# A twelve-stage transformer kernel: the hand-over between two stages in another order, with one weight split of each hand-over in two parts

## The chip, the cores and the metric

The kernel runs on one core of one Trainium2 chip. The metric is the device time of one launch in microseconds; the time given for the kernel before is the median of 3 runs. A profiled execution of the same program gives a trace of every engine, and all durations below are from that one execution.

## The reference, cut to what matters

Twelve residual stages run on x of 256 tokens by 1024 channels, all in float32. Each stage is a normalization, a mixer or a feed-forward block, and a second normalization before the residual addition:

```python
def rms_norm(x, g):
    y = x * lax.rsqrt(jnp.mean(x * x, axis=-1, keepdims=True) + RMS_EPS)
    return y * g

def swiglu(x, w_gate, w_up, w_down):
    return (jax.nn.silu(x @ w_gate) * (x @ w_up)) @ w_down

# first block, for each of two layers
x = x + rms_norm(attention(rms_norm(x, pre), ...), post)
x = x + rms_norm(swiglu(rms_norm(x, pre), ...), post)
# second block, for each of two layers
x = x + 0.5 * rms_norm(swiglu(rms_norm(x, ng[0]), ...), ng[1])
x = x + rms_norm(mixer(rms_norm(x, ng[2])) @ w_out, ng[3])
x = x + rms_norm(memory_xattn(rms_norm(x, ng[4]), mem_n, ...), ng[5])
x = x + 0.5 * rms_norm(swiglu(rms_norm(x, ng[6]), ...), ng[7])
```

The order of the stages is na, ffn, dil, ffn, ffn, rwrt, xa, ffn, ffn, dsa, xa, ffn. The two xa stages attend to a second, normalized input (mem).

## The kernel before, in words

**Weights.** All weights come as one stream of 302 chunks of 128 x 2048 float32 (1 MB each), which SyncE loads into a ring of three buffers (`raw`). A matmul of float32 accuracy is made of three fast ones: every operand is split in a high part and the rest. ScalarE makes the high part of a chunk, `whi` (`act_hi`, L294), and VectorE the rest, `wlo = raw - whi` (`dve_lo`, L301). The first three chunks are split in `first_lo` (L306). `mm3` (L225 to L227) and `mm3t` (L231 to L233) then issue `whi*hi`, `whi*lo` and `wlo*hi`. The semaphores `w_hi` and `w_lo` count split chunks, `w_used` counts chunks that TensorE is done with. The split of chunk g+3 is issued by ScalarE and VectorE in the place of chunk g. SyncE reloads a raw buffer once `w_lo` says that its chunk was split (L1879).

**A stage.** First come the projection chunks: bank `pj` gets two tiles of 128 x 256 per chunk, each a sum over eight k slices of the normalized input (`xh`, `xl`, 128 channels each). Then the output phase (`out_pe`): `AR` (the block's result, high and low parts) times the output weights, two k slices per chunk, summed in four banks `acc[0..3]` of 128 x 512, which are two token halves t by two channel halves h.

**The hand-over between two stages**, which the change touches, happens eleven times. In the order of the data:

1. `last_chunk` in `out_pe` finishes the banks one after another. ScalarE squares and sums each (`post_act`, L406). VectorE runs `post_dve`: `scaled(b)` (L416) multiplies a bank by the gain, `mean(t)` (L421) adds up a half's sums, GpSimd raises them to the power -0.5 (L349), and `added(t, h)` (L428) adds the scaled bank to the residual `xt`. The semaphore `x` of the next stage counts these four additions.
2. TensorE transposes `xt` to channels by tokens (`turn_pe`, L339), one k slice and one token half at a time; `tr` counts finished slices. ScalarE makes `xh` of slice k from it (`pre_hi`, L370, count `hi`), VectorE makes `xl` (`pre_lo`, L392, count `lo`). The mean over channels is applied to the products later, so it is not in this chain: ScalarE squares `xt` (`pre_sq`, L378), VectorE makes the mean (`pre_mean`, L397), GpSimd the power (L344), and TensorE broadcasts it (`bcast_pe`, L355).
3. `slices_pe` runs the first two projection chunks of the next stage slice by slice, so that it can start when the first slice is there: for each k, four calls of `mm3` (two chunks, two halves), that is 12 matmuls of 128 x 256. After slices 0 to 3 it issues the transposes of slices 4 to 7.

All engines run their instructions strictly in the order of the program, and wait at semaphores. VectorE's order in the output phase and the hand-over is: the `wlo` splits of the output phase (`out_dve`), `scaled(0)`, `mean(0)`, `scaled(1)`, `scaled(2)`, `added(0,0)`, `mean(1)`, `scaled(3)`, `added(1,0)`, `added(0,1)`, `added(1,1)`, `pre_lo` of slices 0 to 3, a split of a whole weight chunk, `pre_lo` of slices 4 and 5, `pre_mean`, `pre_lo` of slices 6 and 7.

The last split in `out_dve` is that of chunk 1 of the next stage's projection, the second of the two that `slices_pe` uses; the split inside `post_dve` is that of chunk 2.

**The two hand-overs into an xa stage** differ. There the first chunk of the xa stage multiplies the normalized mem, so its 48 matmuls are used to fill TensorE's waits (`first_keys`, calls of `fill`), and `slices_pe` has only one chunk (n = 1), with a fill after slice 3. In these two, VectorE also makes the low part of the eight mem slices (`mem_dve`, L795) just behind its last split in `out_dve`.

Of the kernel before, what the change touches and what calls it, by code (L numbers as in the profile page):

```python
# [8 lines left out]
P = 128  # L9
D = 1024  # L10
T = 256
KT = D // P
# [6 lines left out]
F32 = mybir.dt.float32  # L19
F32R = mybir.dt.float32r  # L20
I32 = mybir.dt.int32
ALU = mybir.AluOpType
# [61 lines left out]
def build_program(nc, stages, wstream, xin, xtok, memin, memtok, vecs_d, gains_d, consts_d, rpb, small, out):  # L84
    NCH = n_chunks(stages)
    with ExitStack() as ctx:
# [5 lines left out]
        def sem(name):  # L92
            if name not in sems:
                sems[name] = ctx.enter_context(nc.semaphore(name))
            return sems[name]
# [89 lines left out]
        w_hi = sem("w_hi")  # L185
        w_lo = sem("w_lo")
        w_used = sem("w_used")
        pj_free = sem("pj_free")
        x_in = [sem(f"x_in{i}") for i in range(3)]
        vchain = sem("vchain")  # L190
# [105 lines left out]
        def dve_lo(dve, g, gs):  # L296

            if isinstance(g, int) and g + 3 >= NCH:
                return
            dve.wait_ge(w_hi, g + 4)  # L300
            nc.vector.tensor_tensor(wlo[:, gs, :], raw[:, gs, :], whi[:, gs, :].bitcast(F32),  # L301
                                    ALU.subtract).then_inc(w_lo, 1)

        def first_lo(dve, j):
            dve.wait_ge(w_hi, j + 1)
            nc.vector.tensor_tensor(wlo[:, j, :], raw[:, j, :], whi[:, j, :].bitcast(F32),  # L306
                                    ALU.subtract).then_inc(w_lo, 1)

        def out_dve(dve, w, nk, beside=lambda dve, c: None):
            def body(c, g, gs, it, p, ps):  # L310
                dve_lo(dve, g, gs)
                beside(dve, c)
            chunk_loop(dve, w, nk // 2 - 1, body, peel=1, last=True)

# [22 lines left out]
        def turn_pe(pe, t, k):  # L337

            return nc.tensor.transpose(acc[k % 4][:, (k // 4) * T + t * P:(k // 4) * T + (t + 1) * P],  # L339
                                       xt[:, t, k * P:(k + 1) * P], ident)  # L340
# [69 lines left out]
        def post_dve(dve, w, tag, half, nxt):  # L410

            tmp = [Sb[:, 0, :], Sb[:, 1, :], PTb[:, 0, :], PTb[:, 1, :]]

            def scaled(b):
                dve.wait_ge(*at(tag, "sq", b + 1))
                link(dve, nc.vector.scalar_tensor_tensor(tmp[b], acc[b][:, :], half * D ** 0.5,  # L416
                                                         GB[:, (b % 2) * 512:(b % 2 + 1) * 512], ALU.mult, ALU.mult))

            def mean(t):
                dve.wait_ge(*at(tag, "sq", 2 * t + 2))  # L420
                nc.vector.scalar_tensor_tensor(ss[:, 6 + t:7 + t], ss[:, 2 * t:2 * t + 1], D * EPS,  # L421
                                               ss[:, 2 * t + 1:2 * t + 2], ALU.add, ALU.add)\
                    .then_inc(sg(tag, "mv"), 1)

            def added(t, h):
                dve.wait_ge(*at(tag, "rs", t + 1))
                x = xt[:, t, h * 512:(h + 1) * 512]
                nc.vector.scalar_tensor_tensor(x, tmp[2 * t + h], rsc[:, t:t + 1], x, ALU.mult, ALU.add)\  # L428
                    .then_inc(sg(nxt[0], "x"), 1)

            dve.wait_ge(*at(tag, "g", 16))
            scaled(0)
            mean(0)
            scaled(1)
            scaled(2)
            added(0, 0)
            mean(1)
            scaled(3)
            added(1, 0)
            added(0, 1)  # L440
            added(1, 1)
            if nxt[1]:
                for k in range(4):
                    pre_lo(dve, *nxt, k)
            dve_lo(dve, w.g, w.g % 3)
            w.g += 1
            if nxt[1]:
                for k in range(4, 6):
                    pre_lo(dve, *nxt, k)
                pre_mean(dve, nxt[0])  # L450
                for k in range(6, KT):
                    pre_lo(dve, *nxt, k)
                bcast_dve(dve, nxt[0], rP[:, :], nxt[2])

        def out_pe(pe, w, nk, lo_at, tag, ready, nxt, beside=lambda pe, c: None, fill=lambda pe, n, g=0: None,
# [3 lines left out]
            def last_chunk(g):  # L459
                gs, k0 = g % 3, (nk - 2 + kt0) % nk  # L460
                pe.wait_ge(w_lo, g + 1)
                pe.wait_ge(*at(tag, ready, nk))
                for b in range(4):
                    t, h = divmod(b, 2)
                    for kk in range(2):
                        wk = slice(kk * D + h * 512, kk * D + (h + 1) * 512)
                        x = mm3t(acc[b][:, :], whi[:, gs, wk], wlo[:, gs, wk], AR[:, k0 + kk, t * P:(t + 1) * P],
                                 AR[:, lo_at + k0 + kk, t * P:(t + 1) * P], False, kk == 1)
                    if b == 3:
                        x.then_inc(w_used, 1)  # L470
                    else:
                        x.then_inc(sg(post, "ob"), 1)
                if not nxt:
                    return
                fill(pe, 3, g + 1)
                pe.wait_ge(*at(nxt, "x", 1))
                pe.wait_ge(*at(post, "sq", 3))
                for k in range(3):
                    turn_pe(pe, 0, k)
                fill(pe, 4)  # L480
                pe.wait_ge(*at(nxt, "x", 2))
                for k in range(4):
                    if k == 3:
                        turn_pe(pe, 0, k)
                    last = turn_pe(pe, 1, k)
                    last.then_inc(sg(nxt, "tr"), 1)
                fill(pe, 4)

            def body(c, g, gs, it, p, ps):
# [24 lines left out]
        def proj_pe(pe, w, n, tiles):  # L514
# [7 lines left out]
                    after_chunk.pop(0)()  # L522
            chunk_loop(pe, w, n, body, peel=min(n, len(after_chunk)), is_proj=True)

        def slices_pe(pe, w, n=2, fill=lambda pe, n: None):

            tag = split_tag.pop()
            for c in range(n):
                pe.wait_ge(w_lo, w.g + c + 1)
                pe.wait_ge(pj_free, w.p + c + 1)  # L530
            for k in range(KT):
                pe.wait_ge(*at(tag, "lo", k + 1))
                for c in range(n):
                    for half in range(2):
                        last = mm3(pj[(w.p + c) % 3][:, half * T:(half + 1) * T], (w.g + c) % 3, half * KT + k,
                                   xh[:, k, :], xl[:, k, :], k == 0 and half == 0, k == KT - 1)
                    if k == KT - 1:
                        last.then_inc(w_used, 1)
                if k < 4:
                    if k == 0:  # L540
                        pe.wait_ge(*at(tag, "x", 4))
                    turn_pe(pe, 0, k + 4)
                    turn_pe(pe, 1, k + 4).then_inc(sg(tag, "tr"), 1)
                if k == 3:
                    fill(pe, 5)
            w.g += n
            w.p += n
            bcast_pe(pe, tag, rsc[:, 2:4])
# [1604 lines left out]
```

## Time and profile before

| | |
|---|---|
| Median of 3 runs | 2385.3 us (2384.82 to 2387.32) |
| Profiled execution, its own time | 2383.44 us |
| Its span in the trace | 2381.3 us |
| TensorE busy | 2134.6 us (90%), 14826 matmuls |
| VectorE busy | 1442.8 us (61%) |
| ScalarE busy | 946.6 us (40%) |
| GpSimd busy | 27.4 us (1%) |
| Granted TensorE clock, mean | 0.938 |
| DMA | 341.44 MB, mean 143 GB/s |

The span is the time from the first to the last instruction in the trace; the execution's own time is 2.1 us longer. Busy is the time in which an engine ran at least one instruction. The granted clock is 1.00 at 2.4 GHz and 0.50 at 1.2 GHz.

### The profile page before, as it was taken

The numbers are of one execution on the slowest core, as the hardware profiler recorded it, in microseconds if no ns is written. First come the engines' busy times: TensorE is split into PE (matmuls) and PEld (weight loads), VectorE is DVE, ScalarE is ACT, GpSimd is POOL, SyncE is SP. The second block draws the span as 40 slices with busy tenths as digits, with TensorE's granted clock in tenths as the row PEclk, the third lists the DMA queues.
The fourth block names the chain that finished last, engine by engine and source line by source line (L and its number), as shares of the span: only waits on it lengthen the run. The fifth ranks groups of instructions, "written<-read, shape, count | busy, mean of one in ns | idle before, by whom it ended". The sixth has DMA issues, their size and how long they took to land.

```text
span 2381.3 us, 36838 instructions
## 1 busy us (share of the span) xinstructions
PE 2134.6 (90%) x14826; PEld 1958.8 (82%) x14826; DVE 1442.8 (61%) x1982; ACT 946.6 (40%) x1249; POOL 27.4 (1%) x46
## 2 busy tenths in 40 slices
PE   5779999999999999999982998799999996597998
PEld 5668988989878997998972888699799886386997
DVE  4646755555565764774687736577467456565773
ACT  4334444333344444443421315444344333354442
POOL 0000000000000000000000000000000000000000
PEclk8899999999999999999996978899999988898999
DMA  6214554443323554455540004255545542142553
GB/s 270 107 62 150 186 203 151 159 142 107 124 89 115 194 187 175 162 191 196 194 148 11 1 36 151 80 194 178 202 144 192 194 167 103 44 154 70 193 197 112
DMA packets 49787, 341.44 MB, mean 143 GB/s; under 512 B 5776, under 2 KB 6544, under 8 KB 9616
## 3 DMA queue, kind: packets, MB, share of 16 engines
q1 hardware_dynamic: 45648, 324.36, 38.0%
q10 hardware_dynamic: 4032, 15.53, 1.8%
q8 instruction: 82, 1.34, 0.2%
q14 instruction: 25, 0.20, 0.0%
HBM read 338.82 MB, written 1.05 MB: 143 GB/s over the span
## 4 chain that ended last, share of the span: by engine, by line
PE 82%; DVE 12%; issue 2%; ACT 2%; DMA 1%; POOL 0%; DVEq 0%; SPq 0%; POOLq 0%; ACTq 0%
PE pj L225 16%; PE pj L226 16%; PE pj L227 16%; PE acc L231 6%; PE acc L233 6%; PE acc L232 6%; PE acc L569 2%; PE pj L233 2%; PE pj L232 2%; PE pj L231 2%; PE acc L561 2%; PE mb L578 2%; DVE xt L428 1%; DMA raw<-in_wstream 1%; DVE sm L604 1%
## 5 line engine op out<-in xcount | busy, mean ns | idle before, releaser
L301 DVE TENSOR_TENSOR wlo<-raw,whi 128x2048 fp32r<-128x2048 f32 x299 | 685.0, 2291 | 406.5 <-ACT whi L294 406.5
L225 PE MATMUL pj<-xh,whi 128*128 128x256 f32 x3024 | 876.3, 290 | 20.9 <-DVE wlo L306 12.9
L226 PE MATMUL pj<-xl,whi 128*128 128x256 f32 x3024 | 866.8, 287 | 0.0
L227 PE MATMUL pj<-xh,wlo 128*128 128x256 f32 x3024 | 866.3, 286 | 0.0
L294 ACT ACTIVATE whi<-raw 128x2048 fp32r<-128x2048 f32 x299 | 570.5, 1911 | 549.7 <-PE acc L233 239.4
L225 PEld LDWEIGHTS pj<-xh,whi 128*128 128x128 f32 x3024 | 592.4, 196 | 27.4 <-issue 27.4
L226 PEld LDWEIGHTS pj<-xl,whi 128*128 128x128 f32 x3024 | 592.6, 196 | 0.0
L227 PEld LDWEIGHTS pj<-xh,wlo 128*128 128x128 f32 x3024 | 591.8, 196 | 0.0
L231 PE MATMUL acc<-whi,AR 128*128 128x512 f32 x688 | 275.3, 400 | 9.4 <-DVE AR L1768 4.4
L232 PE MATMUL acc<-whi,AR 128*128 128x512 f32 x688 | 273.9, 398 | 0.0
L233 PE MATMUL acc<-wlo,AR 128*128 128x512 f32 x688 | 273.5, 397 | 0.0
L738 ACT ACTIVATE AR<-F 128x256 f32 (+1 forms) x132 | 55.2, 418 | 376.8 <-DVE F L719 376.8
L231 PEld LDWEIGHTS acc<-whi,AR 128*128 128x128 f32 x688 | 130.8, 190 | 41.7 <-issue 4.6
L233 PEld LDWEIGHTS acc<-wlo,AR 128*128 128x128 f32 x688 | 130.5, 190 | 31.6
L232 PEld LDWEIGHTS acc<-whi,AR 128*128 128x128 f32 x688 | 130.7, 190 | 30.8
L561 PE MATMUL acc<-F 64*128 64x128 f32 (+2 forms) x320 | 77.1, 407 | 70.1 <-DVE sm L604 33.4
L561 PEld LDWEIGHTS acc<-F 64*128 64x128 f32 (+1 forms) x320 | 48.6, 213 | 84.7 <-DVE sm L604 39.4
L722 DVE TENSOR_TENSOR AR<-F,AR 128x256 f32 (+1 forms) x132 | 56.2, 426 | 100.5 <-ACT AR L738 100.5
L640 ACT ACTIVATE Sb<-Sb,sm 128x256 f32<-128x256 f32 (+1 forms) x96 | 55.3, 576 | 142.7 <-DVE sm L604 142.4
L711 DVE TENSOR_TENSOR F<-pj,rP 128x512 f32<-128x512 f32 x132 | 90.6, 686 | 0.2
L231 PE MATMUL pj<-whi,xh 128*128 128x256 f32 (+1 forms) x304 | 86.5, 285 | 0.0
L232 PE MATMUL pj<-whi,xl 128*128 128x256 f32 (+1 forms) x304 | 86.5, 284 | 0.0
(324 smaller groups left out, 2063.0 us busy)
## 6 DMA issues: line engine op xcount, KB each, us to landing
raw<-in_wstream SPq DMA_DIRECT2D x302, 1024.0 KB, 4.8
F<-in_gains ACTq DMA_DIRECT2D x12, 512.0 KB, 5.4
F<-in_rpb SPq DMA_DIRECT2D x4, 1024.0 KB, 17.5
F<-in_memtok ACTq DMA_DIRECT2D x2, 1024.0 KB, 4.8
F<-in_memin ACTq DMA_DIRECT2D x2, 1024.0 KB, 7.7
F<-in_small ACTq DMA_DIRECT2D x1, 1536.0 KB, 6.6
F<-in_xin SPq DMA_DIRECT2D x2, 512.0 KB, 6.2
xt<-in_xtok SPq DMA_DIRECT2D x1, 1024.0 KB, 11.3
```

The costliest lines, as they stand in the source:

```text
L225: nc.tensor.matmul(o, wh, k_hi, start=first, stop=False, skip_group_check=True)
L226: nc.tensor.matmul(o, wh, k_lo, start=False, stop=False, skip_group_check=True)
L227: return nc.tensor.matmul(o, wl, k_hi, start=False, stop=last, skip_group_check=True)
L231: nc.tensor.matmul(o, k_hi, wh, start=first, stop=False, skip_group_check=True)
L232: nc.tensor.matmul(o, k_lo, wh, start=False, stop=False, skip_group_check=True)
L233: return nc.tensor.matmul(o, k_hi, wl, start=False, stop=last, skip_group_check=True)
L294: nc.scalar.activation(whi[:, gs, :], raw[:, gs, :], ACT.Copy).then_inc(w_hi, 1)
L301: nc.vector.tensor_tensor(wlo[:, gs, :], raw[:, gs, :], whi[:, gs, :].bitcast(F32), ALU.subtract).then_inc(w_lo, 1)
L561: last = nc.tensor.matmul(b[:, c0:c0 + n], lhsT, rhs, start=True, stop=True)
L640: nc.scalar.activation(S, S, ACT.Exp, bias=sm[:, i:i + 1], accum_out=sm[:, 4 + i:5 + i]).then_inc(sg(tag, "p"), 1)
L711: nc.vector.tensor_tensor(GU.rearrange("p (a t) -> p a t", a=2), pj[ps][:, :].rearrange("p (a t) -> p a t", a=2), rP[:, None, :].to_broadc ...
L722: nc.vector.tensor_tensor(AR[:, bass.ds(c + FT, 1), :] if not isinstance(c, int) else AR[:, c + FT, :], M, (AR[:, bass.ds(c, 1), :] if not ...
```

## The change

- VectorE, output phase: of the last weight split only one half is made there, the columns of k slices 0 to 3 of both tiles (`half_lo` with part 0, 128 x 2 x 512). It is counted by a new semaphore, `w_front`. The other half (part 1) is made in `post_dve`, behind `pre_lo` of slice 3, and only it counts up `w_lo`.
- VectorE, hand-over: `pre_lo` of slice 0 stands ahead of `added(0,1)`, that of slice 1 ahead of `added(1,1)`.
- TensorE, hand-over: the two transposes of slice 3 are moved from `out_pe` to `slices_pe`, behind the matmuls of slice 0 and the wait for the fourth addition.
- TensorE, `slices_pe`: for each k the products with `xh` come first, for all chunks and halves (`whi*xh`, `wlo*xh`), behind a wait for `hi`; then those with `xl`, behind a wait for `lo`. It waits for `w_front` at the start, and for the full split of the second chunk only at k = 4.

The numbers and shapes of the matmuls stay the same. The diff:

```diff
         def out_dve(dve, w, nk, beside=lambda dve, c: None):
             def body(c, g, gs, it, p, ps):
-                dve_lo(dve, g, gs)
+                if isinstance(g, int) and c == nk // 2 - 2 and g + 3 < NCH:
+                    dve.wait_ge(w_hi, g + 4)
+                    half_lo(dve, gs, 0).then_inc(w_front, 1)
+                else:
+                    dve_lo(dve, g, gs)
                 beside(dve, c)
...
+        def half_lo(dve, gs, part):
+
+            v = lambda a: a[:, gs, :].rearrange("p (h x) -> p h x", h=2)[:, :, part * 512:(part + 1) * 512]
+            return nc.vector.tensor_tensor(v(wlo), v(raw), v(whi).bitcast(F32), ALU.subtract)
...
             added(1, 0)
+            if nxt[1]:
+                pre_lo(dve, *nxt, 0)
             added(0, 1)
+            if nxt[1]:
+                pre_lo(dve, *nxt, 1)
             added(1, 1)
             if nxt[1]:
-                for k in range(4):
+                for k in range(2, 4):
                     pre_lo(dve, *nxt, k)
+                half_lo(dve, (w.g - 1) % 3, 1).then_inc(w_lo, 1)
             dve_lo(dve, w.g, w.g % 3)
...
-                for k in range(4):
-                    if k == 3:
-                        turn_pe(pe, 0, k)
-                    last = turn_pe(pe, 1, k)
-                    last.then_inc(sg(nxt, "tr"), 1)
+                for k in range(3):
+                    turn_pe(pe, 1, k).then_inc(sg(nxt, "tr"), 1)
...
             tag = split_tag.pop()
+            if n == 2:
+                pe.wait_ge(w_lo, w.g + 1)
+            fronts[0] += 1
+            pe.wait_ge(w_front, fronts[0])
             for c in range(n):
-                pe.wait_ge(w_lo, w.g + c + 1)
                 pe.wait_ge(pj_free, w.p + c + 1)
             for k in range(KT):
+                if k == 4:
+                    pe.wait_ge(w_lo, w.g + n)
+                pe.wait_ge(*at(tag, "hi", k + 1))
+                for c in range(n):
+                    for half in range(2):
+                        o, wk = pj[(w.p + c) % 3][:, half * T:(half + 1) * T], slice((half * KT + k) * P, (half * KT + k + 1) * P)
+                        for i, a in enumerate((whi, wlo)):
+                            nc.tensor.matmul(o, a[:, (w.g + c) % 3, wk], xh[:, k, :], start=k == 0 and half == 0 and i == 0,
+                                             stop=False, skip_group_check=True)
                 pe.wait_ge(*at(tag, "lo", k + 1))
                 for c in range(n):
                     for half in range(2):
-                        last = mm3(pj[(w.p + c) % 3][:, half * T:(half + 1) * T], (w.g + c) % 3, half * KT + k,
-                                   xh[:, k, :], xl[:, k, :], k == 0 and half == 0, k == KT - 1)
+                        o, wk = pj[(w.p + c) % 3][:, half * T:(half + 1) * T], slice((half * KT + k) * P, (half * KT + k + 1) * P)
+                        last = nc.tensor.matmul(o, whi[:, (w.g + c) % 3, wk], xl[:, k, :], start=False,
+                                                stop=k == KT - 1, skip_group_check=True)
                     if k == KT - 1:
                         last.then_inc(w_used, 1)
                 if k < 4:
                     if k == 0:
                         pe.wait_ge(*at(tag, "x", 4))
+                        turn_pe(pe, 0, 3)
+                        turn_pe(pe, 1, 3).then_inc(sg(tag, "tr"), 1)
                     turn_pe(pe, 0, k + 4)
                     turn_pe(pe, 1, k + 4).then_inc(sg(tag, "tr"), 1)
```

VectorE's order of instructions at the first hand-over (na to ffn), before. `post_sq` counts ScalarE's squares, `post_rs` GpSimd's powers, `pre_hi` the slices of `xh`; F_50 is the arena, here the gain:

```order
L301 TENSOR_TENSOR wlo<-raw,whi 128x2048 [waits w_hi] x3
L416 SCALAR_TENSOR_TENSOR Sb<-acc,F_50 128x512 [waits post_sq,post_g]
...
L428 SCALAR_TENSOR_TENSOR xt<-PTb,rsc,xt 128x512 [waits post_rs,vchain]
L428 SCALAR_TENSOR_TENSOR xt<-Sb,rsc,xt 128x512 [waits post_rs]
L428 SCALAR_TENSOR_TENSOR xt<-PTb,rsc,xt 128x512 [waits post_rs]
L392 SCALAR_TENSOR_TENSOR xl<-acc,vecs,xh 128x256 [waits pre_hi] x4
L301 TENSOR_TENSOR wlo<-raw,whi 128x2048 [waits w_hi]
```

And the same place with the change (L302 is `dve_lo`, L308 `half_lo`, L426 `scaled`, L438 `added`, L402 `pre_lo`):

```order
L302 TENSOR_TENSOR wlo<-raw,whi 128x2048 [waits w_hi] x2
L308 TENSOR_TENSOR wlo<-raw,whi 128x2x512 [waits w_hi]
L426 SCALAR_TENSOR_TENSOR Sb<-acc,F_50 128x512 [waits post_sq,post_g]
...
L438 SCALAR_TENSOR_TENSOR xt<-PTb,rsc,xt 128x512 [waits post_rs,vchain]
L402 SCALAR_TENSOR_TENSOR xl<-acc,vecs,xh 128x256 [waits pre_hi]
L438 SCALAR_TENSOR_TENSOR xt<-Sb,rsc,xt 128x512 [waits post_rs]
L402 SCALAR_TENSOR_TENSOR xl<-acc,vecs,xh 128x256 [waits pre_hi]
L438 SCALAR_TENSOR_TENSOR xt<-PTb,rsc,xt 128x512 [waits post_rs]
L402 SCALAR_TENSOR_TENSOR xl<-acc,vecs,xh 128x256 [waits pre_hi] x2
L308 TENSOR_TENSOR wlo<-raw,whi 128x2x512
L302 TENSOR_TENSOR wlo<-raw,whi 128x2048 [waits w_hi]
```

The third split shrank to a half; the other half, and two of the `xl` instructions, took new places.

TensorE at the same hand-over, from the second group of transposes on, before:

```order
L339 MATMUL acc<-cst,xt 128x128 [waits pre_x]
L339 MATMUL acc<-cst,xt 128x128 x4
L225 MATMUL pj<-xh,whi 128x256 [waits pj_free,w_lo,pre_lo]
L226 MATMUL pj<-xl,whi 128x256
L227 MATMUL pj<-xh,wlo 128x256
...
L339 MATMUL acc<-cst,xt 128x128 [waits pre_x]
```

And with the change (L349 is `turn_pe`, L556 and L562 are the matmuls of `slices_pe`):

```order
L349 MATMUL acc<-cst,xt 128x128 [waits pre_x]
L349 MATMUL acc<-cst,xt 128x128 x2
L556 MATMUL pj<-xh,whi 128x256 [waits pj_free,pre_hi,w_front,w_lo]
L556 MATMUL pj<-xh,wlo 128x256
...
L562 MATMUL pj<-xl,whi 128x256 [waits pre_lo]
L562 MATMUL pj<-xl,whi 128x256 x3
L349 MATMUL acc<-cst,xt 128x128 [waits pre_x]
L349 MATMUL acc<-cst,xt 128x128 x3
```

The first matmul of the next stage waits for a slice of `xh` in the place of one of `xl`, three transposes instead of five stand between the second wait for `x` and it, and four instead of two stand behind slice 0.

## Rows read from the trace of the kernel before

**Rows 1.** The page, part 4: the chain that ended last, by engine.

```profile
PE 82%; DVE 12%; issue 2%; ACT 2%; DMA 1%; POOL 0%; DVEq 0%; SPq 0%; POOLq 0%; ACTq 0%
```

**Rows 2.** Waits of TensorE: who waited for whom, us in total, times, longest us.

```profile
PE acc L339 <- DVE xt L428: 27.6, 20, 2.0
PE pj L225 <- DVE xl L392: 8.1, 9, 1.2
```

**Rows 3.** Timeline of TensorE, first hand-over: start us, us, what, [idle before <-releaser].

```profile
189.79 0.40 PE L233 MATMUL acc<-wlo,AR 128*128 128x512 f32 x1
...
193.40 0.85 PE L339 MATMUL acc<-cst,xt 128*128 128x128 f32 x5 [1.01 <-DVE xt L428]
195.21 0.55 PE L225 MATMUL pj<-xh,whi 128*128 128x256 f32 x1 [0.96 <-DVE xl L392]
...
202.62 0.36 PE L225 MATMUL pj<-xh,whi 128*128 128x256 f32 x1
...
204.28 0.36 PE L225 MATMUL pj<-xh,whi 128*128 128x256 f32 x1
```

**Rows 4.** Timeline of VectorE, first hand-over.

```profile
186.58 2.29 DVE L301 TENSOR_TENSOR wlo<-raw,whi 128x2048 fp32r<-128x2048 f32 x1 [3.31 <-ACT whi L294]
188.79 0.69 DVE L416 SCALAR_TENSOR_TENSOR Sb<-acc,F 128x512 f32<-128x512 f32 x1
...
191.70 0.15 DVE L421 SCALAR_TENSOR_TENSOR ss<-ss 128x1 f32<-128x1 f32 x1
...
192.59 0.75 DVE L428 SCALAR_TENSOR_TENSOR xt<-PTb,rsc,xt 128x512 f32<-128x512 f32 x1
...
193.92 0.75 DVE L428 SCALAR_TENSOR_TENSOR xt<-PTb,rsc,xt 128x512 f32<-128x512 f32 x1
194.58 1.66 DVE L392 SCALAR_TENSOR_TENSOR xl<-acc,vecs,xh 128x256 fp32r<-128x256 f32 x4
```

**Rows 5.** Timeline of ScalarE and GpSimd, first hand-over.

```profile
189.32 0.20 ACT L406 ACTIVATION_READ_ACCUMULATOR F<-acc 128x1 f32 x1
...
190.72 0.19 ACT L406 ACTIVATION_READ_ACCUMULATOR F<-acc 128x1 f32 x1
...
193.76 1.57 ACT L370 ACTIVATE xh<-acc,vecs 128x256 fp32r<-128x256 f32 x4 [1.05 <-PE acc L339]
195.20 1.07 ACT L378 ACTIVATE F<-xt 128x1024 bf16<-128x1024 f32 x1
...
191.93 0.54 POOL L349 TENSOR_TENSOR rsc<-ss,power 128x1 f32<-128x1 f32 x1 [1.64 <-DVE ss L421]
```

**Rows 6.** Windows, TensorE: stretch, length, busy (instructions), granted clock, DMA share, GB/s.

```profile
sum 104.29, PE 104.29; mean PE 14.90
...
sum 27.54, PE 27.54; mean PE 13.77
...
190.19:193.62 3.43, 0.77 (x6) 1.00 0.70 287
...
1525.55:1528.98 3.43, 0.77 (x5) 0.94 0.73 296
...
195.21:200.77 5.56, 5.56 (x26) 0.50 0.19 47
...
1139.82:1142.85 3.03, 3.03 (x15) 0.50 0.02 5
```

**Rows 7.** Timelines at the first hand-over into xa, and one window there.

```profile
1449.26 0.35 PE L225 MATMUL pj<-AR,whi 128*128 128x256 f32 x1 [3.65 <-DVE AR L795]
...
1450.05:1456.88 6.83, 5.16 (x26) 0.50 0.02 10
```

**Rows 8.** The page, parts 5 and 6: two VectorE groups, and the weight loads.

```profile
L301 DVE TENSOR_TENSOR wlo<-raw,whi 128x2048 fp32r<-128x2048 f32 x299 | 685.0, 2291 | 406.5 <-ACT whi L294 406.5
...
L722 DVE TENSOR_TENSOR AR<-F,AR 128x256 f32 (+1 forms) x132 | 56.2, 426 | 100.5 <-ACT AR L738 100.5
...
raw<-in_wstream SPq DMA_DIRECT2D x302, 1024.0 KB, 4.8
```

More of the change, by code:

```diff
@@ L187, in build_program @@
         w_used = sem("w_used")
+        w_front = sem("w_front")
         pj_free = sem("pj_free")
@@ L523, in proj_pe @@
             chunk_loop(pe, w, n, body, peel=min(n, len(after_chunk)), is_proj=True)
+        fronts = [0]
         def slices_pe(pe, w, n=2, fill=lambda pe, n: None):
             tag = split_tag.pop()
+            if n == 2:
+                pe.wait_ge(w_lo, w.g + 1)
+            fronts[0] += 1
+            pe.wait_ge(w_front, fronts[0])
             for c in range(n):
-                pe.wait_ge(w_lo, w.g + c + 1)
                 pe.wait_ge(pj_free, w.p + c + 1)
             for k in range(KT):
+                if k == 4:
[7 more added lines that the diff above has]
+                                             stop=False, skip_group_check=True)
                 pe.wait_ge(*at(tag, "lo", k + 1))
```

## The prediction

> **What bounds the kernel now.** I read the page first. The chain that ended last is TensorE for 82% and VectorE for 12% [rows 1]. So TensorE's matmuls set the time, and what can still be had lies where the chain leaves TensorE. TensorE's waits name the hand-over between stages: its transposes wait for VectorE's additions 27.6 us, and the first matmul for the first slice of `xl` 8.1 us, nine times [rows 2]. There are eleven hand-overs; nine have the plain form, and two lead into an xa stage.
>
> The timelines show one plain hand-over; in the other eight every step has the same distance from the last output matmul within 0.2 us. That matmul ends at 190.19 [rows 3]. ScalarE has squared bank 2 at 189.52 and bank 3 at 190.91 [rows 5]. VectorE was held by a whole weight split until 188.8 [rows 4], so it reaches `mean(1)` only at 191.70, 0.8 us after ScalarE had bank 3. `added(1,0)` starts 0.89 us after that mean, with GpSimd's power between them [rows 4, 5]. It ends at 193.34; the transposes begin at 193.40 [rows 3] and ScalarE's `xh` at 193.76 [rows 5]. But VectorE then has two more additions to do, so `pre_lo(0)` starts at 194.58 [rows 4], although its `xh` was there about 0.4 us earlier. The first matmul of the next stage follows at 195.21: 5.02 us without dense work.
>
> The clock adds a second cost. Behind 195.21 TensorE runs 5.56 us at clock 0.50 [rows 6]. The pass over the eight slices (first matmul to the broadcast) takes 14.90 us on average in seven hand-overs (the row with sum 104.29), and 13.77 us in the two (sum 27.54) where the low clock held for only 3.03 us of the pass [rows 6]. At full clock a slice with transposes takes 204.28 - 202.62 = 1.66 us, and the last four, from 204.28 to the end of the first pass at 195.21 + 14.90 = 210.11, take 1.46 us each [rows 3, 6]. So a pass at full clock would be 4 x 1.66 + 5.83 = 12.47 us, and the clock costs 2.43 us in seven passes and 1.30 us in two.
>
> **The half split.** 2048 columns cost VectorE 2291 ns, 256 cost 426 ns [rows 8]: 1.04 ns per column, so 1024 take about 1.2 us. Bounds: half of 2291, and, should the cut view cost as much as the whole, nothing saved. I take 1.2 us as the shapes lie between these two rows. VectorE then starts `scaled(0)` 1.1 us earlier, at 187.7. It can't keep all of that: `scaled(2)` needs bank 2's square (189.52), `added(0,0)` follows at 190.3, and `mean(1)` needs 190.91. It runs at 191.0 instead of 191.70. `added(1,0)` then starts at 191.9 and ends at 192.6, 0.7 us earlier. If nothing is saved in the split, this 0.7 us is gone.
>
> **The order.** The three transposes follow at 192.7, ScalarE 0.36 us later, and takes about 0.47 us for the first slice: `xh(0)` is there at 193.5. TensorE now waits for that alone and starts at about 193.6, **1.6 us earlier** than 195.21. Of that, 0.7 us come from the half split and 0.9 us from not waiting for `xl`. `pre_lo(0)` runs at 193.5 to 194.0, and the eight `xh` matmuls, 0.95 us at full clock, cover it.
>
> **What is queued behind the new wait.** VectorE now sits at `pre_lo(0)` from 192.6 to 193.5, with two additions behind it. They end at 194.7 and 195.8; before, the fourth ended at 194.67. TensorE waits for the fourth behind slice 0. At full clock slice 0 is done at 193.6 + 1.43 = 195.05, which gives a new wait of **0.8 us**; at half clock slice 0 lasts until 196.2 and the wait is hidden. The two transposes of slice 3 move from a stretch where TensorE waited anyway into the pass: (1.66 - 1.46) = **0.2 us** each time.
>
> ScalarE: `xh(3)` comes at 196.8, two squares of 1.07 us each [rows 5] to 198.9, `xh(4)` at 199.3. VectorE: `xl(3)` at 197.3, second half 198.4, whole split 200.7, `xl(4)` 201.1. TensorE needs these at k = 4, which at full clock begins at 196.2 + 3 x 1.66 = 201.2 and asks for `xl(4)` 0.95 us later. Covered, by 1 us; without that cover, each microsecond that `xl(4)` is late costs one per hand-over. SyncE reloads the second raw buffer when the second half is split, at 198.4 instead of 188.9. The load takes 4.8 us [rows 8] and so ends by 204, also if it shares the DMA with the next one; ScalarE wants the chunk only after the pass, at about 207. Nothing. The 11 extra VectorE instructions (0.15 us each) lie in VectorE's slack. The second wait per slice on TensorE stands at a signal long given: nothing.
>
> **Into xa.** In both, VectorE goes straight from the split to the eight mem slices, and TensorE waits for these, in the first for 3.65 us until 1449.26 [rows 7]. All of it moves by the 1.15 us saved. `xh(0)` comes late there (it stands behind a fill), but the fills keep TensorE in work. I take 1.15 us for each, **2.3 us**.
>
> **The clock.** In seven of the nine stretches from the last output matmul to 3.43 us later, which is when the changed kernel would feed TensorE densely again, the granted clock is still 1.00, as in the first; two read 0.94 and 0.99 [rows 6]. So in most hand-overs the clock fell while TensorE was waiting, after the moment at which it will now be working. And in the two passes with 3.03 us of low clock, dense work began about 0.4 us after the fall; in the seven others the work began later and the low stretch was longer. Both speak for fewer and shorter low stretches. Against it: the wait is still 3.4 us long, and in the first hand-over into xa a wait of 3.65 us was followed by 6.83 us at 0.50 [rows 7].
>
> **The sum.** Without any change in the clock's cost: 9 x (1.6 - 0.2) + 2.3 = 14.9 us. If the clock never fell in a hand-over: plus 7 x 2.43 + 2 x 1.30 = 19.6, plus some 4 in the two into xa (26 instructions at half clock each, about 0.09 us per 256 columns and some of it covered), minus 9 x 0.8 for the new wait: 31.3 us. I take the middle, that half of the clock's cost comes back: 23 us. Against the profiled execution (2383.4 us) that is 2360.4; the median before is 1.9 us higher, so 2362.
>
> A rule weighs against this. The row says that a low stretch costs 2.43 us. The Trainium skill, TensorE: Matmul & The Clock Gate, section Terms, prices a throttled stretch at its whole time times (1 - K/N). For the 6.83 us of [rows 7] that is an estimate of 3.4 us, more than a pass lost here. Both are right where TensorE has nothing to run in a part of the stretch, as before 195.21. By that rule nothing in these passes is saved if the stretch stays where it is, since earlier work only fills it: that is the second rival.
>
> **Rivals.**
> 1. *The clock stays high everywhere*: 31 us, 2354. For it: the seven windows at 1.00. Against: a wait of 3.4 us that is cut only by six short transposes. Chance 0.2.
> 2. *The low stretch stays in place and is now filled.* Of the 1.6 us, 1.26 then lie at half clock and count half: 1.6 - 0.63 - 0.2 = 0.8 us, times nine, plus 2.3: 9.4 us, 2376. For it: seven of nine low stretches were long. Against: the two short ones, and that work now begins before or with the fall. Chance 0.13.
> 3. *The gain is eaten at the fourth addition.* If `xh(0)` comes 0.8 us later than worked out (transposes, ScalarE), TensorE starts later by as much and the additions too, and the half split saves little: nothing remains within 0.2%, 2385. Chance 0.06.
> 4. *Slower*: VectorE's strict order. `pre_lo(0)` holds the additions, these hold slice 3, ScalarE's squares and `xh(4)`, and ahead of `xl(4)` stand now one and a half splits in the place of one. It decides when slice 4's products with `xl` would start later than before, about 205 in the first hand-over, against 201.1 worked out. At 1 us beyond, the nine hand-overs cost 9 us: 2394. Against: it needs 4 us more than the durations of these rows give. Chance 0.05.
>
> The forecast itself has 0.56. **How the numbers follow.** About 0.2% (4.8 us) is what a measurement of this kernel can tell from no change. The forecast and rivals 1 and 2 are faster by more than that: 0.89; rival 3 is the same, 0.06; rival 4 slower, 0.05. The range of 2353 to 2376 takes in rivals 1 and 2 and the bound in which the half split saves nothing (6.3 us less than the sum). It leaves out the two others, 0.11.
>
> **What would show it.** From the last output matmul to the first product of `xh` 3.4 us instead of 5.0; `mean(1)` at the end of ScalarE's fourth square; a wait of VectorE for `xh(0)` of 0.9 us; a wait of TensorE at the transposes behind slice 0 of about 0.8 us where the clock is full, none where it is low; passes of 13.4 to 14.9 us; a mean granted clock above 0.938. I am wrong if TensorE waits for `xl(4)` or for the second half split at k = 4, or if the half split takes near 2.3 us.

## The result, and the profile after

The changed kernel takes 2366.76 us (median of 4 runs, 2362.39 to 2368.56) against 2385.06 us before (4 runs): the ratio is 0.9918, with a 95% interval of 0.9903 to 0.9934, so 18.3 us less. Run again beside the experiments it took 2364.58 us against 2384.05 us, ratio 0.9921 (0.9906 to 0.9937). The forecast was 2362 us in a range of 2353 to 2376.

The page of the changed kernel, parts 1, 4 and 5, against [rows 1, 8]:

```profile
PE 2132.6 (90%) x14826; PEld 1953.1 (83%) x14826; DVE 1442.8 (61%) x1993; ACT 945.2 (40%) x1249; POOL 27.4 (1%) x46
...
PE 83%; DVE 11%; ACT 2%; issue 2%; DMA 1%; POOL 0%; DVEq 0%; SPq 0%; POOLq 0%; ACTq 0%
...
L302 DVE TENSOR_TENSOR wlo<-raw,whi 128x2048 fp32r<-128x2048 f32 x288 | 659.9, 2291 | 365.0 <-ACT whi L295 364.3
```

VectorE's share of the chain went from 12% to 11%; eleven instructions came in, and eleven of the whole splits are gone. The waits of TensorE, against [rows 2]:

```profile
PE acc L349 <- DVE xt L438: 21.9, 21, 2.0
...
PE pj L556 <- ACT xh L380: 3.7, 9, 0.7
```

The first matmul of a stage now waits for ScalarE's `xh`, not for VectorE's `xl`. The timeline of TensorE at the first hand-over, against [rows 3]; the last output matmul ends here at 188.59:

```profile
188.20 0.39 PE L234 MATMUL acc<-wlo,AR 128*128 128x512 f32 x1
189.55 0.55 PE L349 MATMUL acc<-cst,xt 128*128 128x128 f32 x3 [0.96 <-DVE xt L438]
191.11 0.55 PE L349 MATMUL acc<-cst,xt 128*128 128x128 f32 x3 [1.01 <-DVE xt L438]
192.09 0.40 PE L556 MATMUL pj<-xh,whi 128*128 128x256 f32 x1 [0.44 <-ACT xh L380]
...
194.64 1.05 PE L349 MATMUL acc<-cst,xt 128*128 128x128 f32 x4
```

The first product comes 3.50 us behind the last output matmul; before it was 5.02. Of VectorE, against [rows 4], and of ScalarE and GpSimd, against [rows 5]:

```profile
184.98 1.23 DVE L308 TENSOR_TENSOR wlo<-raw,whi 128x1024 fp32r<-128x1024 f32 x1 [3.31 <-ACT whi L295]
...
188.02 0.69 DVE L426 SCALAR_TENSOR_TENSOR PTb<-acc,F 128x512 f32<-128x512 f32 x1 [0.28 <-ACT F L416]
...
189.41 0.15 DVE L431 SCALAR_TENSOR_TENSOR ss<-ss 128x1 f32<-128x1 f32 x1
...
190.30 0.75 DVE L438 SCALAR_TENSOR_TENSOR xt<-PTb,rsc,xt 128x512 f32<-128x512 f32 x1
191.98 0.48 DVE L402 SCALAR_TENSOR_TENSOR xl<-acc,vecs,xh 128x256 fp32r<-128x256 f32 x1 [0.93 <-ACT xh L380]
...
193.44 0.74 DVE L438 SCALAR_TENSOR_TENSOR xt<-PTb,rsc,xt 128x512 f32<-128x512 f32 x1
...
199.55 0.87 DVE L402 SCALAR_TENSOR_TENSOR xl<-acc,vecs,xh 128x256 fp32r<-128x256 f32 x2
```

```profile
189.12 0.19 ACT L416 ACTIVATION_READ_ACCUMULATOR F<-acc 128x1 f32 x1
...
189.64 0.54 POOL L359 TENSOR_TENSOR rsc<-ss,power 128x1 f32<-128x1 f32 x1 [1.88 <-DVE ss L431]
```

The half split takes 1.23 us. `mean(1)` (189.41) follows the fourth square (189.31) within 0.1 us; before it was 0.8 us behind. VectorE then waits 0.93 us for `xh(0)`, and the fourth addition ends at 194.18, 5.6 us behind the last output matmul instead of 4.5. TensorE reaches it later than that, at half clock, and does not wait. The windows of the nine passes (first product to broadcast), against [rows 6], first the one after na, then the one before dil, which is the longest, then the sum:

```profile
192.09:206.32 14.23, 14.23 (x106) 0.88 0.39 149
387.46:402.88 15.42, 15.42 (x106) 0.80 0.45 171
...
sum 127.43, PE 127.43; mean PE 14.16
```

Before they took 131.83 us together (104.29 and 27.54, [rows 6]), 14.65 each. In eight of the nine the clock was low for 3.4 us, in the dil one for 6.8. The nine hand-overs, from the last output matmul to the broadcast, fell from 177.2 to 159.3 us, the two into xa from 40.4 to 38.3: 20.0 us. The span is 17.5 us shorter. The first hand-over also begins 1.6 us earlier, which is scatter: in the other profiles it begins between 188.0 and 193.0 us, in either order. Inside the stages between, 4.1 us were given back, which the second experiment below looks at.

### The profile page after: what moved, and what is told of

Its sections match the earlier page's. It is cut to its first block, busy times and chain, and to the rows that moved or that the text cites. A ratio compares the mean times of both kernels' runs of the same rounds, so it can differ in the third digit from the quotient of the medians.

```text
span 2363.8 us, 36860 instructions
## 1 busy us (share of the span) xinstructions
PE 2132.6 (90%) x14826; PEld 1953.1 (83%) x14826; DVE 1442.8 (61%) x1993; ACT 945.2 (40%) x1249; POOL 27.4 (1%) x46
## 3 DMA queue, kind: packets, MB, share of 16 engines
HBM read 338.82 MB, written 1.05 MB: 144 GB/s over the span
## 4 chain that ended last, share of the span: by engine, by line
PE 83%; DVE 11%; ACT 2%; issue 2%; DMA 1%; POOL 0%; DVEq 0%; SPq 0%; POOLq 0%; ACTq 0%
PE pj L226 14%; PE pj L227 14%; PE pj L228 14%; PE acc L232 6%; PE acc L233 6%; PE acc L234 6%; PE pj L556 4%; PE acc L598 2%; PE pj L234 2%; PE pj L232 2%; PE pj L233 2%; PE pj L562 2%; PE acc L590 2%; PE mb L607 2%; DMA raw<-in_wstream 1%
## 5 line engine op out<-in xcount | busy, mean ns | idle before, releaser
L302 DVE TENSOR_TENSOR wlo<-raw,whi 128x2048 fp32r<-128x2048 f32 x288 | 659.9, 2291 | 365.0 <-ACT whi L295 364.3
L226 PE MATMUL pj<-xh,whi 128*128 128x256 f32 x2704 | 771.8, 285 | 12.6 <-DVE wlo L312 12.6
L227 PE MATMUL pj<-xl,whi 128*128 128x256 f32 x2704 | 767.7, 284 | 0.0
L228 PE MATMUL pj<-xh,wlo 128*128 128x256 f32 x2704 | 767.5, 284 | 0.0
L226 PEld LDWEIGHTS pj<-xh,whi 128*128 128x128 f32 x2704 | 521.8, 193 | 16.5 <-issue 16.5
L227 PEld LDWEIGHTS pj<-xl,whi 128*128 128x128 f32 x2704 | 522.1, 193 | 0.0
L228 PEld LDWEIGHTS pj<-xh,wlo 128*128 128x128 f32 x2704 | 521.6, 193 | 0.0
L556 PE MATMUL pj<-xh,whi 128*128 128x256 f32 x320 | 91.7, 314 | 3.7 <-ACT xh L380 3.7
L556 PE MATMUL pj<-xh,wlo 128*128 128x256 f32 x320 | 86.9, 299 | 0.0
```

Source lines behind the costliest of these rows:

```text
L226: nc.tensor.matmul(o, wh, k_hi, start=first, stop=False, skip_group_check=True)
L227: nc.tensor.matmul(o, wh, k_lo, start=False, stop=False, skip_group_check=True)
L228: return nc.tensor.matmul(o, wl, k_hi, start=False, stop=last, skip_group_check=True)
L556: nc.tensor.matmul(o, a[:, (w.g + c) % 3, wk], xh[:, k, :], start=k == 0 and half == 0 and i == 0, stop=False, skip_group_check=True)
```

## The experiments

"Start" is the time from the last output matmul to the first product of `xh`, "pass" that from there to the broadcast, both as means of the nine plain hand-overs in the profile of that run. The runs were made in three series; the kernel before had medians of 2384.05 us in the first (half split alone, order alone, changed again, added(0,1) first), 2383.96 in the second (the three with extra matmuls) and 2383.74 in the third (the last two rows), and each ratio is to that of its own series.

| Run | Median us | Ratio to before (95%) | Start | Pass |
|---|---|---|---|---|
| before | 2384.05 | | 5.04 | 14.65 |
| changed kernel, again | 2364.58 | 0.9921 (0.9906 to 0.9937) | 3.57 | 13.92 |
| half split alone | 2373.27 | 0.9957 (0.9944 to 0.9970) | 4.35 | 14.64 |
| order alone | 2375.52 | 0.9963 (0.9951 to 0.9976) | 4.28 | 14.44 |
| changed, added(0,1) first | 2365.94 | 0.9927 (0.9915 to 0.9940) | 3.55 | 14.18 |
| changed, extra matmuls | 2355.62 | 0.9885 (0.9868 to 0.9902) | 3.53 | 13.39 |
| both of these | 2351.27 | 0.9861 (0.9846 to 0.9876) | 3.53 | 12.73 |
| before, extra matmuls | 2364.55 | 0.9919 (0.9905 to 0.9932) | 5.04 | 12.44 |
| both, and extra in xa | 2346.90 | 0.9847 (0.9834 to 0.9860) | 3.54 | 12.73 |
| changed, second half split thrice | 2379.15 | 0.9983 (0.9974 to 0.9992) | 3.57 | 15.39 |

### The half split alone, and the order alone

The half split alone, against the kernel before; `slices_pe` waits for `w_front` and, at k = 4, for the full split, as in the change:

```diff
-                dve_lo(dve, g, gs)
+                if isinstance(g, int) and c == nk // 2 - 2 and g + 3 < NCH:
+                    dve.wait_ge(w_hi, g + 4)
+                    half_lo(dve, gs, 0).then_inc(w_front, 1)
+                else:
+                    dve_lo(dve, g, gs)
...
                 for k in range(4):
                     pre_lo(dve, *nxt, k)
+                half_lo(dve, (w.g - 1) % 3, 1).then_inc(w_lo, 1)
             dve_lo(dve, w.g, w.g % 3)
```

The order alone, against the changed kernel; `slices_pe` then waits for the full splits of its chunks at the start, and neither for `w_front` nor again at k = 4:

```diff
-                if isinstance(g, int) and c == nk // 2 - 2 and g + 3 < NCH:
-                    dve.wait_ge(w_hi, g + 4)
-                    half_lo(dve, gs, 0).then_inc(w_front, 1)
-                else:
-                    dve_lo(dve, g, gs)
+                dve_lo(dve, g, gs)
...
-                half_lo(dve, (w.g - 1) % 3, 1).then_inc(w_lo, 1)
```

> Only the half split of the change, in the order of before (pre_lo behind all four additions, slices of mm3, transposes in their old places). My theory: mean(1) runs at the end of the fourth square, 0.7 us earlier, and everything behind it moves by that: first product of xh at 4.3 us behind the last output matmul instead of 5.0, and 1.1 us in the two hand-overs into xa. 9 x 0.7 + 2 x 1.1 = 8.5 us, with up to 4 us more or 2 less from the clock: about 2375 us. Rival (the half split does nothing, the order does all): 2385 us, first product still at 5.0 us.

> Only the order of the change (pre_lo between additions, xh products first, transposes of slice 3 later), with the whole weight split in the output phase as before. My theory: mean(1) stays late, but the first product comes at 4.2 us instead of 5.0; passes 0.2 us longer for the two moved transposes. 9 x (0.9 - 0.2) = 6.3 us, nothing in the hand-overs into xa, with up to 5 us more from a shorter low stretch of the clock: 2374 to 2379 us. Rival (the two parts need each other, since the fourth addition is now later): under 3 us gained, 2382 us or more.

Measured: 10.8 us and 8.5 us less than before. TensorE's timelines, first the half split alone, behind an output phase that ends at 190.40, then the order alone, behind 190.62:

```profile
192.91 0.76 PE L349 MATMUL acc<-cst,xt 128*128 128x128 f32 x5 [1.01 <-DVE xt L438]
194.73 0.55 PE L226 MATMUL pj<-xh,whi 128*128 128x256 f32 x1 [1.05 <-DVE xl L402]
```

```profile
193.82 0.55 PE L345 MATMUL acc<-cst,xt 128*128 128x128 f32 x3 [1.01 <-DVE xt L434]
194.81 0.55 PE L546 MATMUL pj<-xh,whi 128*128 128x256 f32 x1 [0.44 <-ACT xh L376]
```

The starts of this hand-over are 4.33 and 4.19 us, as worked out (4.3 and 4.2). The two parts act on different links of one chain, and their starts add up: 0.69 + 0.76 = 1.45 us against 1.47 and 1.50 for the whole. The times do so too, 10.8 + 8.5 = 19.3 us against 19.5, but each has an interval of about 3 us to both sides, and the half split's 10.8 holds a piece that was not worked out (8.5 us were): in its profile the nine plain hand-overs are 6.3 us shorter, and the two into xa 4.2 where 2.2 were expected, 3.6 of them in the second, in which the clock did not fall in that profile. Both rivals fall.

### The changed kernel again, and the kernel before again

No edit; each gives a second profile. The kernel before took 2381.49 us in its one run.

> The changed kernel itself, once more, for a second profile. The first profile shows 20.0 us gained between the last output matmul and the broadcast of the eleven hand-overs, 1.6 us before the first one, and 5.0 us given back inside the rwrt stage (2.75) and the dsa stage (2.26), which the change does not touch. Theory one, the scatter of the low clock stretches in these stages: in this profile the two stages take other times, by 1 to 4 us, and the hand-overs the same sum within 3 us. Theory two, a later reload or a later split costs time in these stages: both are again 2 to 3 us longer than before.

> The kernel before once more, for a second profile. In three profiles with the changed order the dsa stage took 162.0 us with 51.2 us of low clock, against 159.8 us and 44.4 us in the profile of before. Theory one (scatter of the low stretches): this profile has another time for the dsa stage than 159.8, up to 162. Theory two (the changed order shifts the stage against the clock in a fixed way): again 159 to 160 us.

The rwrt stage (broadcast to last output matmul) took 292.0 us in both profiles of before, and 294.7, then 291.2 us with the change: that loss was scatter. The dsa stage is less clear. Its windows, in the second profile of before and in the second of the change:

```profile
1936.71:2096.85 160.14, 116.09 (x688) 0.84 0.26 91
```

```profile
1922.52:2084.57 162.05, 119.06 (x688) 0.84 0.26 95
```

Its matmuls are the same 688, and the mean clock is 0.84 in both, but TensorE was busy with them 3 us longer. Over all twelve profiles it took 158.8 to 161.8 us with the hand-over in the order of before (four profiles), and 158.9 to 163.6 us in the changed order (eight). What tells the profiles apart is how much matmul work fell into the low stretches of the clock: TensorE was busy for 21.9 to 26.3 us within them in the six profiles of 158.8 to 160.4 us, and for 30.8 to 37.6 us in the six of 161.8 to 163.6. So it is the clock. For rwrt theory one holds. For dsa the two profiles of each kernel agree with each other, as theory two had it, but a fixed shift by the changed order is not what the twelve show: three of the eight are short ones, and one of the four is a long one. Whether the changed order makes the long ones more likely (the middle of the eight, 162.0, is 2 us above that of the four) stays open.

### added(0,1) first

```diff
-            if nxt[1]:
-                pre_lo(dve, *nxt, 0)
             added(0, 1)
+            if nxt[1]:
+                pre_lo(dve, *nxt, 0)
```

> The change with added(0,1) back ahead of pre_lo(0), where VectorE waits 0.93 us for xh(0) and the addition takes 0.67. The fourth addition then ends 0.7 us earlier, the first product stays at 3.5 us. Theory one: with the clock low behind the start, slice 0 takes 2.56 us and hides the fourth addition, so the time is that of the changed kernel within 2 us. Theory two: the fourth addition holds the pass; then 0.5 to 0.8 us per hand-over are gained, 2360 us.

2365.94 us: no difference. VectorE's timeline, behind an output phase that ends at 193.00:

```profile
194.71 0.75 DVE L438 SCALAR_TENSOR_TENSOR xt<-PTb,rsc,xt 128x512 f32<-128x512 f32 x1
195.38 0.74 DVE L438 SCALAR_TENSOR_TENSOR xt<-Sb,rsc,xt 128x512 f32<-128x512 f32 x1
196.39 0.87 DVE L402 SCALAR_TENSOR_TENSOR xl<-acc,vecs,xh 128x256 fp32r<-128x256 f32 x2 [0.27 <-ACT xh L380]
197.18 0.74 DVE L438 SCALAR_TENSOR_TENSOR xt<-PTb,rsc,xt 128x512 f32<-128x512 f32 x1
```

The addition fits into the wait for `xh(0)`, which shrinks from 0.93 to 0.27 us, and the fourth addition ends 4.93 us behind the last output matmul instead of 5.6. Nobody asked for it sooner: TensorE, at half clock for most of slice 0, issues the transposes behind it only at 198.54, 0.6 us after that end. Theory one holds.

### Extra matmuls in the waits

```diff
+        def warm(pe, n):
+            for _ in range(n):
+                nc.tensor.matmul(mb[:, 0:256], ident, cst[:, 0:256], start=True, stop=True)
...
                 fill(pe, 3, g + 1)
+                plain = fill.__defaults__ == (0,) and fill.__name__ == "<lambda>"
+                if plain:
+                    warm(pe, 2)
...
                 fill(pe, 4)
+                if plain:
+                    warm(pe, 2)
                 pe.wait_ge(*at(nxt, "x", 2))
...
                 fill(pe, 4)
+                if plain:
+                    warm(pe, 1)
```

In the kernel before they are three, two and two.

> The changed kernel with extra matmuls in TensorE's waits of the nine plain hand-overs: 128x256 float32 products of constants into the free bank mb, two ahead of the first transposes, two ahead of the second, one behind them; nothing reads them. Their only effect is that TensorE is busy. Theory one (the clock costs 1.35 us per pass, since it falls in the wait, and at full clock the fourth addition would be waited for): the clock stays at 1.00 through the hand-over, passes go from 13.9 to about 13.45 us and show a wait of 0.8 us at the transposes behind slice 0; with starts 0 to 0.2 us later, 2 to 5 us faster than the changed kernel. Theory two (the wait is too short now to cost clock, or the fall has another reason): low stretches as before, time equal or up to 2 us longer.

> The same extra matmuls, and added(0,1) back ahead of pre_lo(0). Theory one: at full clock slice 0 ends 4.9 us behind the last output matmul, just when the fourth addition does, so the 0.8 us wait goes too: passes of about 12.7 us, hand-overs of 16.2 to 16.4 us instead of 17.6, and 9 x 1.2 = 11 us under the changed kernel, about 2354 us. Theory two: no difference to the run with the extra matmuls alone.

> The kernel before with extra matmuls in the waits of the nine plain hand-overs (three, two and two). Nothing of the change is in it. Theory one, the clock cost of 2.43 us in seven passes and 1.30 in two that the prediction worked out: passes of 12.5 us instead of 14.65, 19.6 us less, about 2365 us. Rival: the pass is held by VectorE or ScalarE and not by the clock; under 5 us less.

The windows of the passes. First the changed kernel with the extra matmuls (one pass, and the sum), then with `added(0,1)` first as well, then the kernel before with them:

```profile
193.30:206.65 13.35, 12.88 (x106) 1.00 0.41 158
...
sum 120.51, PE 115.86; mean PE 12.87
```

```profile
195.37:208.04 12.67, 12.67 (x106) 1.00 0.44 167
...
sum 114.54, PE 114.34; mean PE 12.70
```

```profile
195.27:207.70 12.43, 12.43 (x105) 1.00 0.25 86
...
sum 111.94, PE 111.93; mean PE 12.44
```

The granted clock is 1.00 in all 27 passes. In the kernel before this alone is worth 19.4 us (19.6 were expected), as much as the whole change. In the changed kernel a gap opens inside the pass, 13.35 us long with 12.88 busy; its timeline shows the wait that the prediction had worked out for full clock:

```profile
194.33 0.64 PE L573 MATMUL pj<-xl,whi 128*128 128x256 f32 x4
195.44 0.65 PE L349 MATMUL acc<-cst,xt 128*128 128x128 f32 x4 [0.47 <-DVE xt L438]
```

With `added(0,1)` first it is gone in this hand-over (0.19 us are left in the one before dil), and the pass is 0.66 us shorter. So the same edit is worth nothing at half clock and 9 x 0.66 = 5.9 us at full clock (4.4 us in the medians). Where the theory said 2 to 5 us under the changed kernel for the first of these runs, 9 were measured: the sum of the passes fell by 6.9 and 4.8 us against the two profiles of the changed kernel, 1.3 us came in the second hand-over into xa, where the clock no longer fell either, and the remaining 1.7 and 2.3 us lie outside the hand-overs. With `added(0,1)` first 2354 us were expected, 11 under the changed kernel; 13.3 were measured.

### Extra matmuls in the hand-overs into xa

```diff
                 fill(pe, 3, g + 1)
+                if tag in MEM:
+                    pe.wait_ge(*at(MEM[tag], "rb", 1))
+                    warm(pe, 3)
```

> The kernel of the run with extra matmuls and added(0,1) first, with three more extra matmuls in each of the two hand-overs into xa, behind the first fill, where TensorE waits 2.0 us for the first addition. Theory: in the first of the two the clock fell with that wait behind it (matmuls of 256 columns 0.21 us apart instead of 0.12); if it stays up, some 20 products cost 0.09 us less each, 1 to 2 us from that hand-over, nothing from the second, which had full clock already: 2349 to 2350 us. Rival: it falls all the same because of the wait of 2.55 us ahead of the first fill: 2351 us.

2346.90 us, 4.4 us less than the run without. The window of the first of these hand-overs, without and with:

```profile
1430.61:1451.07 20.46, 15.90 (x113) 0.83 0.20 74
```

```profile
1426.60:1444.63 18.03, 14.76 (x119) 1.00 0.23 85
```

It is 2.4 us shorter at full clock, and the second did not change (15.92 and 15.91 us). The theory holds, with 2.4 us for the 1 to 2 expected; the other 2 us are outside both hand-overs and have no cause shown. This is the fastest version: 37 us, 1.5%, under the kernel before.

### The second half split thrice

```diff
-                half_lo(dve, (w.g - 1) % 3, 1).then_inc(w_lo, 1)
+                link(dve, half_lo(dve, (w.g - 1) % 3, 1))
+                link(dve, half_lo(dve, (w.g - 1) % 3, 1))
+                half_lo(dve, (w.g - 1) % 3, 1).then_inc(w_lo, 1)
```

> The changed kernel with the second half split made three times over (same values), to price the work that now stands ahead of xl(4) on VectorE: 2 x 1.15 us more, and two short waits. In the changed kernel xl(4) is there at 200.0 and is asked for at 201.4 in the first hand-over, so the first 1.4 us are covered and about 0.9 to 1.1 us should show as a wait of TensorE in slice 4 of each of the nine plain hand-overs: 8 to 10 us over the changed kernel, about 2375 us. Rival (more slack than I see, as xl is asked for last in a slice): under 3 us.

2379.15 us, 14.6 us over the changed kernel. TensorE in slice 4 of the first hand-over:

```profile
202.09 0.74 PE L564 MATMUL pj<-xl,whi 128*128 128x256 f32 x4 [1.05 <-DVE xl L402]
```

Here is the wait of 1.05 us, at the place that was named. It comes in all eleven hand-overs, 13.7 us in all. The nine plain ones have 10.0 us of it and are 11.3 us longer than in the first profile of the changed kernel. The expectation forgot the two into xa, where the wait is 1.86 us each and which are 5.5 us longer together; that only one chunk instead of two is worked on in a slice there fits, but was not tested. So the slower rival's mechanism is real. It was held off in the changed kernel by cover: the three halves take 3.74 us for the 1.22 of one, and of these 2.5 us about 1.5 did not show in the hand-over above, and 1.0 in the one before dil, at full clock, where the prediction had put 1 us.

This run holds a second answer. In two of its nine plain hand-overs, that before dil and the seventh, the clock stayed at 1.00, though nothing was put into the waits. There TensorE waits for the fourth addition behind slice 0, for 0.83 and 0.48 us; before dil:

```profile
388.11 0.36 PE L558 MATMUL pj<-xh,whi 128*128 128x256 f32 x1 [0.66 <-ACT xh L380]
...
390.61 0.66 PE L349 MATMUL acc<-cst,xt 128*128 128x128 f32 x4 [0.83 <-DVE xt L438]
```

## Why the prediction was right or wrong

**The start.** 1.6 us per plain hand-over was worked out, 1.5 measured (5.04 to 3.54 and 3.57). Its two parts, 0.7 and 0.9, were 0.69 and 0.76 when each was run alone. The half split was put at 1.2 us and took 1.23. Every link came at its time: `mean(1)` at the end of the fourth square, the 0.9 us of VectorE's wait (0.93), the fourth addition at +5.6. The bound for a half split that saves nothing was put at 6.3 us less; the 2.3 us into xa hang on it as well, so it should have been 8.6, still inside the range.

**The moved transposes.** 0.2 us per pass was worked out; 12.70 - 12.44 = 0.26 us at full clock is what the changed pass takes more.

**Into xa.** 2.3 us were worked out, 1.15 in each; 2.1 were measured, but as 0.6 and 1.5, so the sum met by luck. TensorE's waits for the mem slices did fall by 2.3 us together, from 5.2 to 2.9. In the first, though, the clock fell at the same distance behind the last output matmul as before (4.6 us, before 4.5), again for 6.8 us, and TensorE was busy for 5.8 us of that in the place of 5.2: the earlier work filled the low stretch, which is the mechanism of the second rival. In the second the low stretch shrank from 6.8 to 3.4 us.

**The new wait.** 0.8 us at full clock was worked out. With extra matmuls it shows as 0.47 us of idle time, and as 0.66 us when it is taken away; in the two plain hand-overs at full clock of the run with the split made thrice, as 0.83 and 0.48 us. In the changed kernel itself the clock was low behind every start, and half clock hid it, as the text said it would.

**The clock's cost before** was put at 2.43 us in seven passes and 1.30 in two, 19.6 us in all. Taken away by extra matmuls, the passes fell by 14.65 - 12.44 = 2.21 us each, 19.9 us in all, and the time by 19.4. The rule of the Trainium skill (TensorE: Matmul & The Clock Gate, section Terms, throttled time times 1 - K/N) prices the first pass so: 14.90 us at a mean clock of 0.81 hold 5.7 us at half rate, an estimate of 2.8 us; that pass measured 14.90 - 12.43 = 2.5. The rows' own difference was the better price here.

**The clock's share.** "I take the middle, that half of the clock's cost comes back" put 8.2 us (half of 31.3 - 14.9) on top of the 14.9: 6.2 us in the nine plain hand-overs, where the new wait is taken off, and 2 us in the two into xa. In the plain ones 18.8 us were thus worked out (9 x 1.4 + 6.2), and 17.9 and 19.8 measured in the two profiles. The middle was met there, but not by its own parts. Against the pass at full clock with the edit that hides the wait (12.73 us), the changed passes still pay 1.43 and 1.19 us for the clock, where 2.2 were paid before: 7.0 and 9.2 us came back, about 40%, and no wait was taken off. The first terms gave 10.9 and 10.6 us in the place of 12.6. That the two differences cancel is luck.

The argument for the middle was half wrong. The granted clock fell in all nine plain hand-overs of both profiles of the changed kernel, also where it had been 1.00 for the first 3.43 us of the wait before. The prediction took it that the clock would still fall where it fell before; it fell 3.0 to 4.6 us behind the last output matmul before, and 2.5 to 3.7 us behind it with the change. Low stretches became shorter, not fewer: 3.4 us in eight and in nine of nine, against 6.8 in seven of nine. The other argument, that work that begins with the fall raises the clock sooner, fits these profiles: of the low stretches with the half split alone, the three of 3.4 us are those whose first product came at most 0.14 us behind the fall, and it came 0.67 to 1.61 us behind it in the six of 6.8; with the order alone the five short ones have it at most 0.82 us behind, the four long ones 1.44 or more. The long one of the changed kernel (before dil, 0.64 us) shows that this distance alone does not decide.

**Given back.** The sum was 23.1 us; the two profiles of the changed kernel are 17.5 and 18.8 us shorter than that of before, the medians 18.3 and 19.5. Two terms are too high or missing. The clock's 2 us into xa did not come on top of the 2.3. And the prediction had no term for the stages in between: there the span lost 4.1 us in the first profile, of which 2.75 in rwrt were scatter of the clock and some 2 in dsa may be lasting, and 2.6 us in the second. The scatter ahead of the first hand-over (1.6 us gained, 0.5 lost) and in the plain ones makes up the rest.

**The other signs.** The mean granted clock was to rise above 0.938: it is 0.939 and 0.941. Passes of 13.4 to 14.9 us were named: 17 of the 18 are 13.6 to 14.2 us, the one before dil in the first profile is 15.4.

**The rivals.** The clock did not stay high (1). The low stretch did not stay as it was (2) in the plain hand-overs, but it did in the first one into xa. The fourth addition ate nothing (3). The order of VectorE can cost time (4), as the split made thrice shows, but it stayed covered.

## What to carry to other kernels

When a wait between two dense stretches of TensorE is a chain over several engines, follow that chain link by link: each place where an engine in strict order does something else first is a gain of its own, and here the two gains added up. Price the clock apart from the wait, and try a few products into a free bank in the wait: here they gave as much as the reordering, and another 9 us on top of it. An edit that measures nothing may be hidden behind a low clock; try it again when the clock is up.

## What was not expected

- Waits of 0.96, 1.01 and 0.44 us with six transposes between them (3.5 us in all) still lost the clock in 18 of 18 plain hand-overs in two profiles; the same waits with five small float32 products in them lost it in none of 18 (two runs). The waits alone do not settle it: in the run with the split made thrice, with the same start, the clock fell in seven of nine.
- Those products cost nothing: the start stayed at 3.53 us, against 3.54 without.
- The extra matmuls of the kernel before made all nine passes alike to 0.01 us (12.43 or 12.44), where they had spread from 13.74 to 15.14.
